# Scaling the softmax's probabilities on ScalarE, head by head, instead of on VectorE

## The reference

```python
m = jnp.maximum(jnp.max(s, axis=-1, keepdims=True), sink)
p = jnp.exp(s - m)
denom = jnp.sum(p, axis=-1, keepdims=True) + jnp.exp(sink - m)
return jnp.einsum('...hgqs,...shd->...qhgd', (p / denom).astype(v.dtype), v)
```

## Time and profile before

| | |
|---|---|
| median of 3 runs | 1076.64 us (1076.58 to 1077.65) |
| the profiled execution's own time | 1077.56 us |
| its span in the trace | 1075.7 us |
| TensorE matmul busy | 1069.9 us, 99% |
| VectorE busy | 714.9 us, 66% |
| ScalarE busy | 586.2 us, 54% |
| GpSimd busy | 483.7 us, 45% |

### The profile page before, as it was taken

How to read it: one execution, slowest core, us unless ns; L and a number is a source line. 1 busy time by engine, 2 the same in 40 slices (tenths; PEclk the granted TensorE clock), 3 DMA queues, 4 the chain that set the end, 5 groups by cost and what they waited for, 6 DMA issues and landing times.

```text
span 1075.7 us, 21059 instructions
## 1 busy us (share of the span) xinstructions
PE 1069.9 (99%) x8755; PEld 1052.9 (98%) x8755; DVE 714.9 (66%) x1020; ACT 586.2 (54%) x895; POOL 483.7 (45%) x377
## 2 busy tenths in 40 slices
PE   9999999999999999999999999999999999999999
PEld 9999999999999999999999999999999999999998
DVE  7598999456785655565549789694577765555542
ACT  7564755777456444444446657467774564444431
POOL 2789865773732111101187879658736321111000
PEclk9999999999999999999999999999999999999999
DMA  9755553544555766455544455434554755555552
GB/s 296 244 172 172 157 176 118 146 151 151 175 175 192 201 215 185 163 174 170 175 143 149 157 173 180 158 120 149 165 156 138 233 167 168 162 172 164 173 173 84
DMA packets 65055, 182.54 MB, mean 170 GB/s; under 512 B 17057, under 2 KB 21793, under 8 KB 64289
## 3 DMA queue, kind: packets, MB, share of 16 engines
q1 hardware_dynamic: 63952, 177.12, 52.7%
q10 hardware_dynamic: 1008, 4.08, 1.0%
HBM read 174.90 MB, written 7.27 MB: 169 GB/s over the span
## 4 chain that ended last, share of the span: by engine, by line
PE 98%; DVE 1%; DMA 1%; ACT 0%; issue 0%; SPq 0%; ACTq 0%
PE ps L457 31%; PE ps L462 30%; PE ps L458 30%; DVE x_lo L1675 1%; DMA raw<-in_w_z 1%; PE ps L607 0%; PE ps L477 0%; PE ps L560 0%; PE ps L774 0%; PE ps L657 0%; PE ps L472 0%; PE ps L679 0%; PE ps L745 0%; PE ps L500 0%; PE ps L538 0%; PE ps L582 0%
## 5 line engine op out<-in xcount | busy, mean ns | idle before, releaser
L457 PE MATMUL ps<-x_hi,w_hi 128*128 128x288 f32 x1952 | 583.5, 299 | 1.9 <-DVE x_lo L1675 1.8
L458 PE MATMUL ps<-x_lo,w_hi 128*128 128x288 f32 x1952 | 575.8, 295 | 0.0
L462 PE MATMUL ps<-x_hi,w_lo 128*128 128x288 f32 x1952 | 574.0, 294 | 0.0
L1780 POOL TENSOR_TENSOR w_lo<-raw,w_hi 128x512 fp32r<-128x512 f32 x258 | 366.9, 1452 | 131.8 <-ACT w_hi L930 131.3
L930 ACT ACTIVATE w_hi<-raw 128x1024 fp32r<-128x1024 f32 x314 | 325.8, 1051 | 144.0 <-PE ps L462 128.8
L457 PEld LDWEIGHTS ps<-x_hi,w_hi 128*128 128x128 f32 x1952 | 365.8, 187 | 9.5 <-issue 5.2
L462 PEld LDWEIGHTS ps<-x_hi,w_lo 128*128 128x128 f32 x1952 | 367.5, 188 | 0.0
L458 PEld LDWEIGHTS ps<-x_lo,w_hi 128*128 128x128 f32 x1952 | 366.6, 188 | 0.4
L1296 DVE TENSOR_TENSOR w_lo<-raw,w_hi 128x1024 fp32r<-128x1024 f32 x185 | 230.3, 1246 | 119.5 <-ACT w_hi L930 119.5
L1805 POOL TENSOR_TENSOR work<-work,rs 128x288 f32<-128x288 f32 x44 | 35.8, 813 | 237.3 <-ACT work L1257 237.3
L462 PE MATMUL ps<-h_hi,w_lo 128*128 128x288 f32 x352 | 104.4, 296 | 0.0
(11 more groups left out here) (249 smaller groups left out, 1044.9 us busy)
## 6 DMA issues: line engine op xcount, KB each, us to landing
raw<-in_w_up SPq DMA_DIRECT2D x88, 512.0 KB, 4.1
raw<-in_w_z SPq DMA_DIRECT2D x66, 512.0 KB, 3.6
raw<-in_w_gate SPq DMA_DIRECT2D x64, 512.0 KB, 3.6
raw<-in_w_branch SPq DMA_DIRECT2D x32, 512.0 KB, 3.5
raw<-in_w_down SPq DMA_DIRECT2D x32, 512.0 KB, 3.6
raw<-in_w_out SPq DMA_DIRECT2D x16, 512.0 KB, 3.6
raw<-in_w_down SPq DMA_DIRECT2D x16, 384.0 KB, 3.2
kv<-in_state ACTq DMA_DIRECT2D x2, 1024.0 KB, 5.7
```

The lines of the kernel that those rows point to most:

```text
L457: pe.matmul(out, wh, rh, start=start, stop=False)
L458: pe.matmul(out, wh, rl, start=False, stop=False)
L462: return pe.matmul(out, w_lo[:, slot, u * UNIT:(u + 1) * UNIT], rh, start=False, stop=stop)
L1780: ins = pool.tensor_tensor(w_lo[:, slot, cols], raw[:, slot, cols], w_hi[:, slot, cols].bitcast(f32), ALU.subtract)
```

## The change

VectorE keeps the sums and the reciprocals of the softmax (now signalled as `shares0`, `shares1` and `shares_s`) and the transposes. The multiplication is made by ACT, one instruction a head, with the reciprocal as a scale that is read from SBUF. ACT signals it by a second count on `exp0`, `exp1` and `exp_s`. Two steps are new on ACT, `scale0` after tile 29's turn and `scale_s` after tile 33's, `decay_exp` moves from step 35 to 36, and the runs of the convolution on VectorE are dealt out otherwise. TensorE's instructions are the same in number and order, and only one of its waits has another name.

```diff
-    conv1=48, exp_s=30, probs_s_turned=34, ...
-    v_copied=39, decay_exp=35, ...
+    conv1=48, exp_s=30, scale0=29, scale_s=33, probs_s_turned=34, ...
+    v_copied=39, decay_exp=36, ...
-CONV_RUNS = (8, 1, 0, 0, 0, 2, 0, 0, 0, 3, 6, 14, 3, 2, 3, 4, 4, 5, 2, 4, 9, 10, 8, 9, 10, 7, 3,
+CONV_RUNS = (8, 1, 0, 0, 0, 2, 0, 0, 2, 2, 7, 4, 8, 3, 2, 3, 4, 5, 2, 4, 9, 10, 8, 9, 10, 7, 3,
...
-                pe.wait_ge(E("probs_s"), l1)
+                pe.wait_ge(E("exp_s"), 2 * l1)
...
+                def scaled(probs, col, at_h, n, signal):
+                    for h in range(at_h, at_h + n):
+                        ins = act.activation(probs[:, h, :], probs[:, h, :], ACT.Copy, scale=small[:, 4, col + h:col + h + 1])
+                    if at_h + n == probs.shape[1]:
+                        ins.then_inc(E(signal), 1)
...
+                        yield from at("scale0")
+                        act.wait_ge(E("shares0"), l1)
+                        scaled(prob0, 0, 0, 8, "exp0")
                         yield from at("exp_s")
...
+                yield from at("scale_s")
+                act.wait_ge(E("shares_s"), l1)
+                scaled(prob_s, 16, 0, 2, "exp_s")
+                act.wait_ge(E("shares1"), l1)
+                scaled(prob1, 8, 0, 4, "exp1")
+                yield
+                scaled(prob1, 8, 4, 4, "exp1")
                 yield from at("probs_s_copied")
...
-                link(dve.reciprocal(small[:, 4, cols], small[:, 3, cols]), l)
-                n, m = probs.shape[1], probs.shape[2]
-                dve.tensor_tensor(probs, probs, small[:, 4, cols].unsqueeze(2).to_broadcast([P, n, m]), ALU.mult)\
-                    .then_inc(E(event), 1)
+                dve.reciprocal(small[:, 4, cols], small[:, 3, cols]).then_inc(E(event), 1)
```

More of the change, by code:

```diff
@@ L101 @@
     exp0=20, exp1=31, prompt_pv=36, prompt_od=37, smp_scores=27, conv0=40,
-    conv1=48, exp_s=30, probs_s_turned=34, probs_s_copied=35, smp_pv=36, smp_od=37, decay_in=24, decay_y=16, decay_log=17,
-    v_copied=39, decay_exp=35, att_in=38, k_copied=41, gelu=46, chunks=41, smp_old=33, old_out=44, smp_out=47,
+    conv1=48, exp_s=30, scale0=29, scale_s=33, probs_s_turned=34, probs_s_copied=35, smp_pv=36, smp_od=37, decay_in=24, decay_y=16, decay_log=17,
+    v_copied=39, decay_exp=36, att_in=38, k_copied=41, gelu=46, chunks=41, smp_old=33, old_out=44, smp_out=47,
     gla_o=37, cv_mean=49, cv_sq=50, smp_update0=57, smp_update1=58, gla_sums=52, gla_rstd=52, cv_var=39, r_silu=54,
@@ L107 @@
     in1=66, in2=66, in3=73, v_turn=38, k_turn=40)
-CONV_RUNS = (8, 1, 0, 0, 0, 2, 0, 0, 0, 3, 6, 14, 3, 2, 3, 4, 4, 5, 2, 4, 9, 10, 8, 9, 10, 7, 3,
-             8, 2, 0, 4, 5, 2, 0, 0, 0, 3, 3, 7, 3, 2, 3, 4, 4, 0, 6, 7, 4, 13, 0, 11, 13, 7, 3)
+CONV_RUNS = (8, 1, 0, 0, 0, 2, 0, 0, 2, 2, 7, 4, 8, 3, 2, 3, 4, 5, 2, 4, 9, 10, 8, 9, 10, 7, 3,
+             8, 2, 0, 4, 5, 2, 0, 0, 1, 2, 3, 2, 5, 3, 2, 3, 4, 0, 6, 7, 4, 13, 0, 11, 13, 7, 3)
 STORES_PER_LAYER = 9
@@ L1423, in softmax_in, with softmax_out @@
                     .then_inc(E(event), 1)
-            def softmax_out(l, l1, cols, probs, event):
+            def softmax_out(l, l1, cols, event):
                 link(dve.tensor_tensor(small[:, 3, cols], small[:, 3, cols], small[:, 2, cols], ALU.add), l)
-                link(dve.reciprocal(small[:, 4, cols], small[:, 3, cols]), l)
-                n, m = probs.shape[1], probs.shape[2]
-                dve.tensor_tensor(probs, probs, small[:, 4, cols].unsqueeze(2).to_broadcast([P, n, m]), ALU.mult)\
-                    .then_inc(E(event), 1)
+                dve.reciprocal(small[:, 4, cols], small[:, 3, cols]).then_inc(E(event), 1)
             def mixers(l, l1, conv_steps):
@@ L1488, in mixers @@
                 yield
-                dve.wait_ge(E("exp0"), l1)
-                softmax_out(l, l1, slice(0, 8), prob0, "probs0")
-                dve.wait_ge(E("probs0"), l1)
+                dve.wait_ge(E("exp0"), 2 * l + 1)
+                softmax_out(l, l1, slice(0, 8), "shares0")
+                yield
+                dve.wait_ge(E("exp_s"), 2 * l + 1)
+                softmax_out(l, l1, slice(16, 18), "shares_s")
+                dve.wait_ge(E("exp0"), 2 * l1)
                 dve.transpose(prob0_t, prob0).then_inc(E("probs0_turned"), 1)
                 yield
-                dve.wait_ge(E("exp_s"), l1)
-                softmax_out(l, l1, slice(16, 18), prob_s, "probs_s")
+                dve.wait_ge(E("exp1"), 2 * l + 1)
+                softmax_out(l, l1, slice(8, 16), "shares1")
                 yield
-                dve.wait_ge(E("exp1"), l1)
-                softmax_out(l, l1, slice(8, 16), prob1, "probs1")
-                dve.wait_ge(E("probs1"), l1)
+                dve.wait_ge(E("exp1"), 2 * l1)
                 dve.transpose(prob1_t, prob1).then_inc(E("probs1_turned"), 1)
```

## The result

The changed kernel takes 1081.43 us (median of 5 runs, 1079.12 to 1081.60); the kernel before has a median of 1077.63 us over 5 runs. The ratio is 1.0032, with an interval of 1.0020 to 1.0043: slower by 0.3%. Three of the five runs lie at 1081.4 to 1081.6 us and two at 1079.1 and 1079.6; the profile is of one of the three, and what follows explains that one. The profiled run took 1081.43 us with a span of 1079.6 us, against 1077.56 and 1075.7 before, so 3.9 us more in both. 2.7 us were forecast. The granted clock was 1.0 in both, the level of 2.4 GHz.

The account below looks back on a forecast made before the run. TensorE was taken to bound the kernel; stalls of 1.35 and 1.34 us at tile 31, all else 0, made 2.7 us, taking the median from 1076.64 to 1079.3 us. The range was 1077.6 to 1081.2 us.

Parts of the forecast that it names:

- ScalarE without overlap: Rival: each scaling holds ACT for its whole duration, 0.39 us, stalling 2.1 us a layer; 1080.9 to 1081.5 us; chance 0.09.
- What bounds the kernel: Whole kernel: TensorE, busy 1069.9 us, bounds it and waits for nothing in the softmax; relieving VectorE alone gains nothing.
- Removed, gain 0: Softmax on VectorE: multiplications of 1.23 and 3.29 us a layer and a smaller one go; TensorE did not wait, gain 0.
- The rival of VectorE's saving coming through: Rival: time saved on VectorE removes TensorE's 1.8 us of waits at the input projection; 1074.8 us at best; chance 0.02.
- Block 0, start of the scalings: First layer's softmax on ACT: scalings wait for VectorE's reciprocal, ending at 115.75, and begin at 115.82 us.
- The price of a scaling: Block 0 on ACT: 0.29 us for each 128-column scaling, 2.34 us for eight; ends 0.11 and 0.39 us each.
- the cheap scaling: Rival: a block 0 scaling takes 0.20 us, not 0.29; 0.6 us a layer, 1077.9 us; chance 0.05.
- The stall at tile 31: TensorE waits for tile 29's drain, delayed behind block 0's scalings: 1.35 us first layer, 1.34 us second.
- The rule on multiplications: Skill rule against multiplying on ScalarE: block 0 takes 2.34 us against 1.23, a loss of 1.1 us a layer, 2.2 in all.
- The rest, the value product, POOL: Other scalings, later drains, value product, decay_exp, POOL's w_lo and loads: later, but covered by room; cost 0.
- The early reciprocal: Rival: VectorE passes its waits, shares0 ready at 113.7, tile 31 on time; 1076.6 us, no slower; chance 0.06.
- The sum: Whole kernel: the two layers' stalls at tile 31, 1.35 + 1.34, add up to 2.7 us.

Follow-up runs that it names:

- both edits: Changed kernel, four convolution steps put back before the second layer's last state step, block 0's scalings moved behind tile 29's drain: 1077.22 us, ratio 0.9999.
- early reciprocal: Changed kernel, block 0's sum and reciprocal moved ahead of block 1's scores on VectorE, four convolution steps put back in the second layer: 1076.52 us, ratio 1.0002.
- without the wait: Changed kernel, block 0's eight scalings in place but by a constant column, not waiting for VectorE's reciprocal: 1077.66 us, ratio 1.0011.
- with half the work: Changed kernel, wait for the reciprocal kept, only four of block 0's eight scalings made: 1078.11 us, ratio 1.0016.
- the added wait: GpSimd waits for VectorE's eighth second-layer x_lo before block 11's low part; ratios 1.0000 (both edits), 1.0002 (early reciprocal), 1.0001 (kernel before).

## Why the prediction came out as it did

The direction was right, 2.7 of the 3.9 us were there for the reason given, and the size of the whole was short: 1081.43 us lies 0.2 us over the upper end of the range, which had been set by another mechanism, ScalarE without overlap, that did not occur. Part of the 2.1 us between the forecast of 1079.3 and the result is the base: the median of before was 1076.64 us over the three runs that the prediction started from and 1077.63 over five. From the profiled execution the prediction went to 1080.3, and 1.1 us are missing there.

- *What bounds the kernel*: right. TensorE is busy 99%, VectorE's 16 us less bring nothing. With the stalls removed (both edits; early reciprocal) the ratio to before is 1.
- *Removed, gain 0*: right, by the same two runs. The rival of VectorE's saving coming through is excluded.
- *Block 0, start of the scalings*: right. Forecast 115.82, measured 115.97, of which 0.18 is the later start of this execution.
- *The price of a scaling*: right. 0.29 forecast from the earlier trace rows, 2.46 us for eight measured (2.34 plus the last one's 0.1 of tail). Neither the cheap scaling nor the one without overlap. Four fewer brought the drain 1.24 us forward, 0.07 of it because that execution ran earlier.
- *The stall at tile 31*: right in both layers, 1.35 and 1.34 forecast, 1.36 and 1.35 measured. That the hundredths agree is luck: from the drain's end to TensorE's start it was 0.14 us and not 0.07 (118.81 to 118.95), and the second matmul followed 0.07 us later than usual and not 0.11. The stall's condition is shown from both sides: without the wait nothing is left of it, and with half the work 0.2 us.
- *The rule on multiplications* of the page "ScalarE: Activation LUTs" in the Trainium skill, section "Rules for kernel authors": wants them on VectorE, the faster engine for each element. The trace agrees on the engines' times (2.46 us on ScalarE, 1.23 on VectorE), but the runs show that these did not decide: the same eight scalings on ScalarE cost 2.7 us in the two layers at one place and nothing one tile later.
- *The rest, the value product, POOL*: cost 0, right. No other drain has a wait behind it, and the decay exponentials begin at 136.99 us where about 137 was forecast.
- *The early reciprocal*: did not happen, as argued; the reciprocal stood in its old place, ending at 115.93, 0.18 later as all of this execution. Of the two long steps ahead of it only the first has two inputs in SBUF; the second, a `TENSOR_SCALAR`, has one, so what the prediction says of two inputs does not cover it, though it too ends with GpSimd's instructions (115.36 and 115.34).
- *The sum*: the step that failed. "Sum: 1.35 + 1.34 = 2.7 us" has no term for the convolution runs dealt anew. The prediction used the new list once, for the 14 instructions (seven steps, which it calls 14 steps) ahead of block 1's transpose in the first layer, and did not count the steps up to the last state step, where the second layer's line of the list matters (the extract of the diff ahead of the prediction shows the first layer's line alone; the second layer's stands in the diffs of the run with four steps put back, for the changed kernel, and of the one with four taken away, for the kernel before): 50 before and 51 now in the first layer, 50 and 46 in the second. Four steps of two instructions at 0.40 us (from the earlier trace rows) are 3.2 us, and the room in the trace of before was 1.67 us. Both numbers could be had; the term would have come to 1.5 us, and the forecast to 4.2; measured were 1.27 and 3.9. The run with four steps put back and the one with four steps taken from the kernel before show the cause from either side.
- Regaining 0.29 us between the layers was not forecast, and could not be from one profile: 0.26 of it is the short wait at 329 us that the profiled execution of before happened to have.
- The two runs at 1079.1 and 1079.6 us stay unexplained. Without the wait at 570 us, worth 1.04 us, a run with all three stalls would take about 1080.4.

## What to carry to other kernels

Work handed to an engine that also drains for TensorE is priced by the drain behind it: add the wait for its input to its duration, take off the time that the engine idled there anyway, and compare the rest with the room. Here the same work one tile later cost nothing. When a change also edits a table that deals filler work, count the table up to each point at which someone waits, in every layer, and compare each difference with the room there. An edit that looks like bookkeeping cost here nearly as much as one of the two stalls that the change was about (1.27 against 1.35 us).

## What the runs showed of the hardware

TensorE's third wait for `x_lo`, at 570 us, stands in some profiles and not in others, though no edit but the last touches that stretch. There VectorE's last three `x_lo` meet GpSimd's low part of a weight. VectorE and GpSimd in the kernel before, which has the wait:

```profile
568.23 2.39 DVE L1675 SCALAR_TENSOR_TENSOR x_lo<-work,prm,x_hi 128x288 fp32r<-128x288 f32 x3
...
568.92 2.85 POOL L1780 TENSOR_TENSOR w_lo<-raw,w_hi 128x512 fp32r<-128x512 f32 x2 [3.84 <-ACT w_hi L930]
```

The kernel with both edits, which has not:

```profile
568.09 1.37 DVE L1690 SCALAR_TENSOR_TENSOR x_lo<-work,prm,x_hi 128x288 fp32r<-128x288 f32 x3
...
568.80 1.80 POOL L1795 TENSOR_TENSOR w_lo<-raw,w_hi 128x512 fp32r<-128x512 f32 x1 [3.87 <-ACT w_hi L930]
```

With the two starting 0.69 or 0.71 us apart, it is once VectorE that loses 1.0 us (2.39 against 1.37 for three) and once GpSimd that loses 0.5 (1.80, where it takes 1.28 with the added wait). All nine profiles without that added wait fall into these two kinds: the last `x_lo` takes 1.53 us in five of them and 0.51 in four, while GpSimd's record starts 0.14 to 0.17 us ahead of it in every one. So these two engines hold each other off here where no semaphore is between them. The Trainium skill, page "SBUF — State Buffer", section "Who interferes with whom", says that the one which issues first holds the other off; both traces agree that one of them is held off, and what decides between starts so close no run here shows.

On one chip the 31 runs of the kernel before lie in two groups about 1.1 us apart (17 at 1076.2 to 1076.7, 13 at 1077.3 to 1077.8 and one at 1075.3); on another chip all 33 lie at 1076.9 or less. The wait at 570 us, worth 1.04 us, fits that distance. That it is the cause is not shown, and it cannot be the only one: two kernels with GpSimd made to wait still had 5 of 22 runs above 1077.0.
